# Splitting the last round's Fourier rows early, taking the second tile's statistic first, and giving all low parts of h to VectorE

## The chip, the cores and the metric

One core of a Trainium2 chip runs the whole kernel. The metric is the device time of one execution in microseconds (us). The kernel before was timed in three executions.

## The reference

A latent stream x (1024 tokens, width 1024) and a context stream (256 tokens) go through two layers. Cut to what bears on the change:

```
# layer 0, per stream; z = h @ w_in gives u, g, f, gf, each 1024 wide
r   = rglru_bidirectional(conv(u))                 # "r rows" of the mix
f   = fourier_mix(f, w_f, b_f)                     # "f rows" of the mix
mix = concatenate([r * silu(g), f * silu(gf)])     # 2048 wide
y   = mix @ w_out                                  # the first out-projection
x   = x + gate * rms_norm(y, g_post)
# layer 1 begins
h   = rms_norm(x, g_pre1) * (1 + scale1) + shift1
z   = h @ w_in1                                    # projections of layer 1
# then rotary, windowed attention with context keys, gate, out-projection, norm, residual
```

All of it is float32.

## The kernel before

**High and low parts.** TensorE takes each float32 operand as two parts of type fp32r, and every product is three matmuls: high by high, high by low, low by high. A high part is a copy with rounding by ScalarE (ACT); a low part is `raw - high`, a tensor_tensor by VectorE (DVE) or GpSimd (POOL). Most of what stands between a DMA and a matmul is this pair.

**Layer 0.** `mixers` (from L414) runs eight rounds, one for 128 channels each. A round makes one row block of r (tile `H` in the buffer `work`) and one of f (tile `xf`), and stores them to the DRAM tensor `mixT` (16 row blocks, of 128 channels by 1280 tokens). The body of the last round also starts the out-projection: L900 finishes f, L905 and L908 finish r, and between them stand calls of the out-projection's `weight_lo`.

**First out-projection** (`out_projection0`, L1118). Ten tiles of 128 tokens; each is a product of 16 blocks (8 of r, then 8 of f) of six matmuls, `half_product` (L1485) doing eight blocks. Tiles 0 and 1 are different: `first_pair` (L1459) walks the 16 weight rows in the order `K_ORDER` (L1109), which is r blocks 0 to 6, f blocks 0 to 6, then the last r block and the last f block, and tile 1 follows tile 0 at a distance of three blocks (`LAG`), so each weight row is split while PE works on others. Weight row i waits for `weight_lo(i)`. Block 7 in this order is the first that needs the f half of `mixT`: `ml[1]`.

Queues around it, each in program order:

- SP (DMA issues) loads the two r halves of tiles 0 and 1 (L1224, `load_first_mix`), weights 0 to 9, stores the last f rows (`store_f`), loads weight 10, waits until that store has landed, then loads the two f halves (L1239, L1240; all eight f row blocks from `mixT`), weight 11, `store_r`, and the rest. Each tile's raw rows use a slot of `mraw`.
- ACT: `weight_hi` 3 to 6, `mixed_hi(0, 1)` (tile 0, f half), `weight_hi` 7, `mixed_hi(1, 1)`, the last r rows straight from `H` (`last_r`), weights 8 to 15.
- DVE: weights 4 and 5, sum and product that finish r (L905, L908), then `weight_lo` 6, `mixed_lo(0, 1)`, 7, `mixed_lo(1, 1)`, `last_r`, 8 to 15.

After a tile's product comes its epilogue: ACT takes the sum of squares of Y and the root (L1315, L1317), DVE scales (L1375), POOL adds x (L1431), ACT takes the squares and the root again (L1323, L1325), DVE writes `xn` (L1386), PE transposes it to `TP` (L1502), DVE multiplies by the gain into `hb` (L1390), POOL adds the shift (L1433), SP stores h (L1213). The body of tile t on ACT and POOL is: split mix tile t+1 (r half, f half), then the epilogue of tile t-1. On SP: load mix tile t+1, load x tile t, store tile t-1; tile 3's mix is loaded by body 2, which comes after tile 0's h is stored. PE: the two half products of tile t, then the transposes of t-1.

**Projections of layer 1** (`projections1`, L1526). The stored h is read back in ten tiles through four slots; ACT makes `h_hi` (L1637), and the low parts are shared: tiles 2, 5 and 8 by POOL (L1743), the others by DVE (L1694), kept apart by `pool_share`, `dve_share` and `wait_low` (from L1091). Slot reuse waits for the low of the tile four back. PE's first slab product is cut in three chunks: tokens of tiles 0 to 3, 4 to 7, 8 and 9, each waiting for its lows. POOL also makes the lows of the first two weight slabs (L1732), the second one after h tile 5.

Of the kernel before, what the change touches and what calls it, by code (L numbers as in the profile page):

```python
# [413 lines left out]
def mixers(nc, a, h_hi, h_lo, work, cols, silu_c, gs, ident, mods, wraw, w_hi, w_lo, gf_hi, gf_lo, slab, W, W4, before,  # L414
           home, h1_ld, w1_ld):
    ctx = ExitStack()
    with ctx:
        def sb(name, shape, dt=F32):
# [44 lines left out]
        r7h, r7l = sem("last_r_hi"), sem("last_r_lo")  # L463
# [6 lines left out]
            nc, a, mods, home, ident, H, h1_ld, w1_ld,  # L470
            Freed(wl, s_gf, s_g, gp_, dft, mp, uv, us, yd, sg, mr, mf, mrs, mfs, gst, ge, r7h, r7l, slot_ld))
# [251 lines left out]
        def _(dve):  # L723
# [23 lines left out]
            def body(t, first, last):  # L747
# [367 lines left out]
Freed = namedtuple("Freed", "wl s_gf s_g gate_products dft mod_sums uv us yd sg mr mf mrs mfs gates_stored gate_rows r7_hi r7_lo slot_loaded")  # L1115


def out_projection0(nc, a, mods, home, ident, H, h1_ld, w1_ld, freed):  # L1118
# [42 lines left out]
    def loops(eng, body):  # L1161

        body(1, 1, False)
        with eng.Fori(1, LT // 2) as j:
# [14 lines left out]
    def sync(sp, store_f, store_r, store_gates):  # L1179
# [4 lines left out]
        def load_first_mix(t, h, slot):  # L1184
            n = KT - 1 if h == 0 else KT
            sp.dma_start(mraw[:, slot, 0:n], a["mixT"][h * KT:h * KT + n, :, t * P:(t + 1) * P]
                         .rearrange("k p n -> p k n")).then_inc(m_ld[slot], 16)
# [36 lines left out]
        load_first_mix(0, 0, 0)  # L1224
        load_first_mix(1, 0, 1)
# [25 lines left out]
        sp.wait_ge(freed.mrs, 16 * KT)  # L1251
        load_mix(2, 0)
# [24 lines left out]
    def scalar(act):  # L1277
        def mixed_hi(t, h):
            slot = t if h == 0 else 1 - t
            act.wait_ge(m_ld[slot], 16 * h + 16)  # L1280
# [4 lines left out]
            n = KT - 1 if h == 0 else KT  # L1285
            nc.scalar.activation(m_hi[t][:, h, 0:n], mraw[:, slot, 0:n], ACT.Copy).then_inc(mh[h], 1)

        def last_r():
            act.wait_ge(freed.mr, KT)
            for t in range(2):  # L1290
                nc.scalar.activation(m_hi[t][:, 0, KT - 1], H[:, t * P:(t + 1) * P], ACT.Copy).then_inc(freed.r7_hi, 1)

        def weight_hi(i):
# [5 lines left out]
            elif i == 10:  # L1299
                act.wait_ge(freed.r7_lo, 2)  # L1300
                act.wait_ge(freed.mrs, 16 * KT)
# [26 lines left out]
        def body(t, s, last):  # L1328
            if not last:
                split(t + 1, 1 - s, 0)  # L1330
                split(t + 1, 1 - s, 1)
            epilogue(t - 1, 1 - s)
# [16 lines left out]
    def vector(dve):  # L1349
# [6 lines left out]
        def mixed_lo(t, h):  # L1356
            slot = t if h == 0 else 1 - t
            n = KT - 1 if h == 0 else KT
            dve.wait_ge(mh[h], t + 1)
            tt(m_lo[t][:, h, 0:n], mraw[:, slot, 0:n], v32(m_hi[t][:, h, 0:n]), ALU.subtract).then_inc(ml[h], 1)  # L1360

        def last_r():
            for t in range(2):
                dve.wait_ge(freed.r7_hi, t + 1)
                tt(m_lo[t][:, 0, KT - 1], H[:, t * P:(t + 1) * P], v32(m_hi[t][:, 0, KT - 1]),
                   ALU.subtract).then_inc(freed.r7_lo, 1)
# [53 lines left out]
    def gpsimd(pool):  # L1420
# [6 lines left out]
        def epilogue(t, s):  # L1427
            w = 1 if is_ctx(t) else 0
            pool.wait_ge(x_ld, 16 * t + 16)
            pool.wait_ge(yn, t + 1)  # L1430
            tt(x1[:, s, :], x1[:, s, :], xt[:], ALU.add).then_inc(xd, 1)  # L1431
            pool.wait_ge(hg, t + 1)
            tt(hb[:, s], hb[:, s], mods[:, SHIFT1, w, :].unsqueeze(2).to_broadcast([P, KT, P]), ALU.add).then_inc(hd, 1)  # L1433

        def body(t, s, last):
            if not last:
                split(t + 1, 1 - s, 0)
                split(t + 1, 1 - s, 1)
            epilogue(t - 1, 1 - s)
# [7 lines left out]
    def tensor(pe, gate_rows):  # L1447
# [11 lines left out]
        def first_pair():  # L1459
            def step(t, i):  # L1460
# [8 lines left out]
                elif k == KT - 1:  # L1469
                    pe.wait_ge(freed.r7_lo, t + 1)  # L1470
                if t == 0:
# [54 lines left out]
def projections1(nc, a, kd_hi, kd_lo, vs, early, h_ld, w_ld):  # L1526

    ctx = ExitStack()
    with ctx:
# [20 lines left out]
        hh, hl = sem("h1_hi_done"), [sem("h1_lo0"), sem("h1_lo1")]  # L1550
# [29 lines left out]
        def _(sp):  # L1580
# [5 lines left out]
            for i in range(2, TT):  # L1586
                if i >= 4:
                    wait_low(sp, hl, i - 4)
# [3 lines left out]
            for i in range(TT - 4, TT):  # L1592
                wait_low(sp, hl, i)
# [133 lines left out]
        def _(pool):  # L1727
# [813 lines left out]
```

## Time and profile before

| | us |
|---|---|
| median of three executions | 1505.27 |
| lowest and highest | 1505.14, 1509.27 |
| the profiled execution | 1508.78 |
| its span, first to last instruction | 1507.0 |
| PE busy with matmuls | 1392.4 (92%) |
| DVE, ACT, POOL busy | 849.5, 736.1, 545.8 |
| mean granted TensorE clock | 0.974 |

Times in the rows are microseconds from the start of the span. A timeline row gives start, duration, engine, source line, operation, output and input, and in brackets the idle time ahead of it with what ended it. The profiled execution lies 1.8 us over its own span and 3.5 us (0.2%) over the median.

### The profile page before, as it was taken

Reading aid. Unit: us, or ns where it says so; the run is one execution under the profiler, and the core shown is the slowest. Engines: PE = TensorE matmul, PEld = TensorE weight load, DVE = VectorE, ACT = ScalarE, POOL = GpSimd, SP = SyncE. Lnnn points to the kernel's source line nnn. Section 1 sums busy time; section 2 is a strip of 40 time slices with the busy share of each in tenths; the row PEclk is TensorE's granted clock in tenths of the full one; section 3 lists DMA queues with packets and bytes.
Section 4 is the critical chain, followed back from the end, with each engine's and each line's share of the span. In section 5 each row is a group of like instructions: output and inputs, shape, how many; then the busy total and the mean of one; then the engine's idle time right before and its main releaser. Section 6 shows DMA issues by size and latency. Waiting matters only on the chain. (4 is left out here: it accounts for less than half of the span.)

```text
span 1507.0 us, 20164 instructions
## 1 busy us (share of the span) xinstructions
PE 1392.4 (92%) x7212; PEld 1161.1 (77%) x7212; DVE 849.5 (56%) x1231; ACT 736.1 (49%) x1149; POOL 545.8 (36%) x260
## 2 busy tenths in 40 slices
PE   5999999999999999989899957999996899998897
PEld 4778888888888888867788846888885788887676
DVE  7788767676776768751111225122221789997532
ACT  5475828273737464732122213222221899997511
POOL 0023232323222223203343414343542666667542
PEclk9999999999999999999999977999998999999999
DMA  9323122222121212372344334724335533241584
GB/s 380 138 70 111 60 92 72 79 75 90 61 90 61 90 61 78 116 252 83 114 115 120 98 110 171 182 84 139 111 104 140 177 121 106 77 147 52 178 231 125
DMA packets 94886, 179.45 MB, mean 119 GB/s; under 512 B 10448, under 2 KB 56944, under 8 KB 92528
## 3 DMA queue, kind: packets, MB, share of 16 engines
q1 hardware_dynamic: 94832, 178.74, 36.9%
q8 instruction: 33, 0.54, 0.2%
q14 instruction: 21, 0.17, 0.0%
HBM read 123.65 MB, written 45.11 MB: 112 GB/s over the span
## 5 line engine op out<-in xcount | busy, mean ns | idle before, releaser
L962 PE MATMUL slab<-h_hi,w_hi 128*128 128x512 f32 x720 | 258.0, 358 | 3.2 <-DVE h_lo L316 2.6
L964 PE MATMUL slab<-h_hi,w_lo 128*128 128x512 f32 x720 | 257.3, 357 | 0.0
L963 PE MATMUL slab<-h_lo,w_hi 128*128 128x512 f32 x720 | 257.2, 357 | 0.0
L931 POOL TENSOR_TENSOR w_lo<-wraw,w_hi 128x1024 fp32r<-128x1024 f32 x29 | 73.8, 2545 | 311.6 <-ACT w_hi L567 311.6
L2092 POOL TENSOR_TENSOR probs<-probs,rdenom 128x2560 f32<-128x2560 f32 (+1 forms) x32 | 135.7, 4241 | 58.1 <-DVE rdenom L2051 58.1
L962 PEld LDWEIGHTS slab<-h_hi,w_hi 128*128 128x128 f32 x720 | 135.5, 188 | 26.0 <-DVE h_lo L316 2.9
L1772 PE MATMUL slab<-h_hi,w_hi 128*128 128x512 f32 (+1 forms) x352 | 135.6, 385 | 18.9 <-DVE h_lo L1694 18.9
L963 PEld LDWEIGHTS slab<-h_lo,w_hi 128*128 128x128 f32 x720 | 135.5, 188 | 22.0
L964 PEld LDWEIGHTS slab<-h_hi,w_lo 128*128 128x128 f32 x720 | 135.5, 188 | 22.0
L1774 PE MATMUL slab<-h_hi,w_lo 128*128 128x512 f32 (+1 forms) x352 | 135.2, 384 | 0.0
L1773 PE MATMUL slab<-h_lo,w_hi 128*128 128x512 f32 (+1 forms) x352 | 135.1, 384 | 0.0
L2068 DVE TENSOR_TENSOR pt_lo<-TB,pt_hi 128x512 fp32r<-128x512 f32 x152 | 104.3, 686 | 32.8 <-ACT pt_hi L2010 26.5
L1970 ACT ACTIVATE probs<-probs,neg_max 128x640 f32<-128x640 f32 (+1 forms) x128 | 102.7, 802 | 23.2 <-DVE neg_max L2043 18.9
L2043 DVE CUSTOM_DVE_ANT_0 probs<-S,mask,nsink 128x640 f32<-128x640 f32 (+1 forms) x128 | 107.6, 842 | 1.7 <-PE S L2125 1.4
L743 DVE SCALAR_TENSOR_TENSOR E<-wm,silu_bcast 128x1024 f32<-128x1024 f32 x64 | 99.8, 1560 | 5.4 <-DMA wm<-in_wm 2.1
L2124 PE MATMUL S<-kd_hi,q_parts 128*128 128x256 f32 (+2 forms) x256 | 89.3, 353 | 13.4 <-DMA q_parts<-qT 12.3
L2164 PEld LDWEIGHTS TB<-ident,probs 128*128 128x128 f32 x608 | 75.9, 141 | 24.0 <-issue 3.7
L2164 PE MATMUL TB<-ident,probs 128*128 128x128 f32 x608 | 91.5, 273 | 2.9 <-DVE pt_lo L2068 1.5
L1772 PEld LDWEIGHTS slab<-h_hi,w_hi 128*128 128x128 f32 x352 | 67.3, 191 | 32.6 <-issue 16.7
L2010 ACT ACTIVATE pt_hi<-TB 128x512 fp32r<-128x512 f32 x152 | 89.2, 587 | 5.8 <-PE TB L2164 5.0
L1773 PEld LDWEIGHTS slab<-h_lo,w_hi 128*128 128x128 f32 x352 | 67.2, 191 | 12.8
L1774 PEld LDWEIGHTS slab<-h_hi,w_lo 128*128 128x128 f32 x352 | 67.1, 191 | 12.8
(321 smaller groups left out, 3184.2 us busy)
## 6 DMA issues: line engine op xcount, KB each, us to landing
wraw<-in_w_in SPq DMA_DIRECT2D x32, 512.0 KB, 3.3
wm<-in_wm SPq DMA_DIRECT2D x32, 512.0 KB, 3.5
mixT<-work SPq DMA_DIRECT2D x16, 640.0 KB, 4.0
mraw<-mixT SPq DMA_DIRECT2D x18, 512.0 KB, 5.4
wm<-in_wm SPq DMA_DIRECT2D x8, 1024.0 KB, 16.2
q_parts<-qT SPq DMA_DIRECT2D x32, 256.0 KB, 4.6
oT<-o_out SPq DMA_DIRECT2D x8, 1024.0 KB, 5.3
work<-in_xT SPq DMA_DIRECT2D x8, 640.0 KB, 8.6
```

The source lines that it names most:

```text
L743: nc.vector.scalar_tensor_tensor(out=E[:, 0:D], in0=wm1[:, q % 2, :], scalar=0.5, in1=silu_b[:, w, :], op0=ALU.mult, op1=ALU.mult, accum_o ...
L962: nc.tensor.matmul(out, l_hi, r_hi, start=start, stop=False)
L963: nc.tensor.matmul(out, l_hi, r_lo, start=False, stop=False)
L964: return nc.tensor.matmul(out, l_lo, r_hi, start=False, stop=stop)
L1772: nc.tensor.matmul(out, w_hi[:, j, k, :], rhs_hi, start=(k == 0), stop=False)
L1773: nc.tensor.matmul(out, w_hi[:, j, k, :], rhs_lo, start=False, stop=False)
L1774: last = nc.tensor.matmul(out, w_lo[:, j, k, :], rhs_hi, start=False, stop=(k == KT - 1))
L1970: nc.scalar.activation(r, r, ACT.Exp, bias=nm[:, u, h:h + 1], scale=-1.0, accum_out=rsum[:, u, h:h + 1]).then_inc(ed, 1)
L2043: nc.vector.tensor_tensor_reduce(out=row(b, pr[:, u, h, :]), in0=S[:, j % 2, at:768], in1=m, scale=-SCALE, scalar=nsink[:, j:j + 1], op0=A ...
L2068: tt(pt_lo[:, x, :], TB[:, tb_bank(b, u, x), :], v32(pt_hi[:, x, :]), ALU.subtract).then_inc(pl, 1)
L2092: nc.gpsimd.tensor_tensor(rows, rows, rden[:, u, :].unsqueeze(2).to_broadcast(rows.shape), ALU.mult).then_inc(pn, 1)
L2164: last = nc.tensor.transpose(TB[:, tb_bank(b, u, x), h * P:(h + 1) * P], pr[:, u, h, x * P:(x + 1) * P], ident[:])
```

## The change

Four edits.

1. In the last round the f halves of tiles 0 and 1 are also only seven row blocks, those stored by earlier rounds, so they no longer wait for the store of the last f rows. SP loads tile 0's f half right behind weight 2 and tile 1's behind weight 6. The eighth f rows come from `xf` as the eighth r rows come from `H` (`last_rows`, with semaphore `f7_lo`). ACT and DVE take these splits earlier: ACT after weights 4 and 5, DVE one between weights 4 and 5 inside the mixer's last round and one ahead of weight 6.
2. Body 1 of the epilogue loops: ACT takes the statistics of tiles 0 and 1 one behind the other, ahead of the split of tile 3; POOL adds x for tiles 0 and 1 ahead of the shift of tile 0. One more pair of bodies is written out for it.
3. SP's body t loads x tile t first, then mix tile t+2 (was t+1), then stores tile t-1.
4. All ten lows of h in `projections1` go to DVE, under one semaphore; POOL splits the second weight slab right behind the first.

```diff
@@ last round, VectorE
                     weight_lo(4)
+                    mixed_lo(0, 1)
                     weight_lo(5)
@@ SP
         load_w(2)
+        sp.wait_ge(m0l, 1)
+        sp.wait_ge(freed.mfs, 16 * (KT - 1))
+        load_first_mix(0, 1)
         sp.wait_ge(freed.s_g, 3 * KT)
-        for i in range(3, 10):
+        for i in range(3, 7):
+            load_w(i)
+        sp.wait_ge(ml[0], 1)
+        load_first_mix(1, 1)
+        for i in range(7, 10):
             load_w(i)
         store_f()
         load_w(10)
-        sp.wait_ge(freed.mfs, 16 * KT)
-        sp.wait_ge(m0l, 1)
-        sp.wait_ge(ml[0], 1)
-        load_first_mix(0, 1, 1)
-        load_first_mix(1, 1, 0)
         load_w(11)
         store_r()
...
         def body(t, s, last):
-            if not (isinstance(t, int) and t == 1) and not last:
-                load_mix(t + 1, 0)
-                load_mix(t + 1, 1)
             load_x(t)
+            if not (isinstance(t, int) and t >= TT - 2):
+                load_mix(t + 2, 0)
+                load_mix(t + 2, 1)
             store(t - 1, 1 - s)
@@ ScalarE
+        def last_rows():
+            act.wait_ge(freed.mf, KT)
             act.wait_ge(freed.mr, KT)
+            for h, rows in enumerate((H, xf)):
+                for t in range(2):
+                    nc.scalar.activation(m_hi[t][:, h, KT - 1], rows[:, t * P:(t + 1) * P],
+                                         ACT.Copy).then_inc(freed.rows_hi, 1)
...
         def body(t, s, last):
+            if isinstance(t, int) and t == 1:
+                split(2, 0, 0)
+                split(2, 0, 1)
+                epilogue(0, 0)
+                epilogue(1, 1)
+            else:
+                if not last:
+                    split(t + 1, 1 - s, 0)
+                    split(t + 1, 1 - s, 1)
+                if not (isinstance(t, int) and t == 2):
+                    epilogue(t - 1, 1 - s)
 
         def rest():
-            for i in range(3, 7):
+            weight_hi(3)
+            weight_hi(4)
+            mixed_hi(0, 1)
+            weight_hi(5)
+            mixed_hi(1, 1)
+            for i in range(6, 10):
                 weight_hi(i)
-            mixed_hi(0, 1)
-            weight_hi(7)
-            mixed_hi(1, 1)
-            last_r()
-            for i in range(8, K2):
+            last_rows()
+            for i in range(10, K2):
                 weight_hi(i)
@@ VectorE
         def rest(copy_gates):
-            weight_lo(6)
-            mixed_lo(0, 1)
-            weight_lo(7)
             mixed_lo(1, 1)
-            last_r()
-            for i in range(8, 12):
+            for i in range(6, 10):
+                weight_lo(i)
+            last_rows()
+            for i in range(10, 12):
                 weight_lo(i)
             copy_gates()
@@ GpSimd
+            if isinstance(t, int) and t == 1:
+                split(2, 0, 0)
+                split(2, 0, 1)
+                residual(0, 0)
+                residual(1, 1)
+                shifted(0, 0)
+            else:
+                if not last:
+                    split(t + 1, 1 - s, 0)
+                    split(t + 1, 1 - s, 1)
+                if not (isinstance(t, int) and t == 2):
+                    residual(t - 1, 1 - s)
+                shifted(t - 1, 1 - s)
@@ projections1, VectorE
-            for i in dve_share(TT):
+            for i in range(TT):
                 at = slice(i * P, (i + 1) * P)
                 dve.wait_ge(hh, i + 1)
-                tt(h_lo[:, :, at], h_tile(i), v32(h_hi[:, :, at]), ALU.subtract).then_inc(hl[1], 1)
+                tt(h_lo[:, :, at], h_tile(i), v32(h_hi[:, :, at]), ALU.subtract).then_inc(hl, 1)
@@ projections1, GpSimd
             split(0, 0)
-            for i in pool_share(TT):
-                at = slice(i * P, (i + 1) * P)
-                pool.wait_ge(hh, i + 1)
-                tt(h_lo[:, :, at], h_tile(i), v32(h_hi[:, :, at]), ALU.subtract).then_inc(hl[0], 1)
-                if i == 5:
-                    split(1, 0)
+            split(1, 0)
             pool.wait_ge(par, 48)
```

## Rows read from the trace of the kernel before

**Rows 1.** Waits by engine and line, PE, 600 to 950 us.

```profile
PE slab L1772 <- DVE h_lo L1694: 18.9, 2, 16.3
PE TP L1502 <- DVE xn L1386: 15.2, 2, 8.3
PE Y L1454 <- DVE wo_over_h L1354: 4.5, 1, 4.5
```

**Rows 2.** Windows: length, busy of PE, PEld, DVE, ACT, POOL, granted clock, DMA.

```profile
657.40:663.40 6.00, 6.00 (x14) 4.74 (x15) 5.93 (x7) 5.39 (x6) 0.00 (x0) 0.50 0.50 201
722.90:725.00 2.10, 2.10 (x7) 1.72 (x6) 1.23 (x1) 0.00 (x0) 0.36 (x1) 0.54 0.15 59
725.00:884.60 159.60, 159.60 (x716) 130.05 (x716) 23.82 (x34) 32.05 (x54) 58.08 (x26) 1.00 0.35 106
```

**Rows 3.** SP's timeline, the two f halves of the first pair.

```profile
649.49 1.00 SPq L1186 DMA_DIRECT2D mraw<-mixT  x2
```

**Rows 4.** VectorE's timeline in the first pair.

```profile
643.78 1.21 DVE L1354 TENSOR_TENSOR wo_over_h<-early,wo_over_h 128x1024 fp32r<-128x1024 f32 x1
...
648.11 1.22 DVE L1354 TENSOR_TENSOR wo_over_h<-early,wo_over_h 128x1024 fp32r<-128x1024 f32 x1
654.89 1.23 DVE L1360 TENSOR_TENSOR m_parts<-mraw,m_parts 128x1024 fp32r<-128x1024 f32 x1 [5.56 <-ACT m_parts L1286]
656.04 1.22 DVE L1354 TENSOR_TENSOR wo_over_h<-early,wo_over_h 128x1024 fp32r<-128x1024 f32 x1
```

**Rows 5.** PE's timeline, a stall in round 0 with its next matmul.

```profile
122.04 0.50 PE L962 MATMUL W<-pq_hi,ab_hi 128*128 128x512 f32 x1 [2.18 <-DVE pq_lo L873]
122.38 0.39 PE L963 MATMUL W<-pq_lo,ab_hi 128*128 128x512 f32 x1
```

**Rows 6.** PE's timeline, the transposes of tiles 1, 2 and 4.

```profile
721.33 1.97 PE L1502 MATMUL TP<-ident,xn 128*128 128x128 f32 x8 [8.32 <-DVE xn L1386]
...
746.11 1.03 PE L1502 MATMUL TP<-ident,xn 128*128 128x128 f32 x8
...
792.28 1.03 PE L1502 MATMUL TP<-ident,xn 128*128 128x128 f32 x8
```

**Rows 7.** Timelines of SP, ACT and POOL ahead of the stall at 721 us.

```profile
705.94 1.21 SPq L1195 DMA_DIRECT2D mraw<-mixT  x2
...
710.49 1.06 ACT L1310 ACTIVATE m_parts<-mraw 128x1024 fp32r<-128x1024 f32 x1 [16.91 <-DMA mraw<-mixT]
...
711.63 4.67 POOL L1425 TENSOR_TENSOR m_parts<-mraw,m_parts 128x1024 fp32r<-128x1024 f32 x2 [6.41 <-ACT m_parts L1310]
```

**Rows 8.** VectorE's timeline: hb of tile 0, scaling of tile 1, its xn.

```profile
702.02 1.22 DVE L1390 TENSOR_TENSOR hb<-TP,mods 128x1024 f32<-128x1024 f32 x1 [7.45 <-PE TP L1502]
...
714.92 1.28 DVE L1375 SCALAR_TENSOR_TENSOR x_tiles<-Y,st,gpb 128x1024 f32<-128x1024 f32 x1
...
720.52 0.75 DVE L1386 TENSOR_SCALAR xn<-x_tiles,st 128x1024 f32<-128x1024 f32 x1
```

**Rows 9.** A steady tile: its xn on DVE, the next mix split on ACT.

```profile
788.98 0.75 DVE L1386 TENSOR_SCALAR xn<-x_tiles,st 128x1024 f32<-128x1024 f32 x1
...
802.00 1.06 ACT L1310 ACTIVATE m_parts<-mraw 128x1024 fp32r<-128x1024 f32 x1 [13.26 <-DMA mraw<-mixT]
```

**Rows 10.** PE's timeline, chunks 0 and 1 of layer 1's first slab.

```profile
910.83 0.77 PE L1772 MATMUL slab<-h_hi,w_hi 128*128 128x512 f32 x1 [16.31 <-DVE h_lo L1694]
...
921.60 0.47 PE L1772 MATMUL slab<-h_hi,w_hi 128*128 128x512 f32 x1 [2.64 <-DVE h_lo L1694]
```

**Rows 11.** VectorE's timeline, the first two lows of h together.

```profile
903.74 5.82 DVE L1694 TENSOR_TENSOR h_lo<-early,h_hi 128x1024 fp32r<-128x1024 f32 x2 [6.70 <-ACT h_hi L1637]
```

**Rows 12.** Windows, the slow stretch in chunk 1 (columns as in rows 2).

```profile
922.80:926.30 3.50, 3.50 (x10) 2.70 (x9) 1.98 (x1) 0.00 (x0) 0.89 (x1) 0.51 0.14 36
```

**Rows 13.** Loads of h tiles: median landing; issue of tile 7; its high.

```profile
early<-hT SPq DMA_DIRECT2D x6, 512.0 KB, 4.2
...
910.71 0.33 SPq L1589 DMA_DIRECT2D rope_swap<-hT  x1
...
917.19 1.06 ACT L1637 ACTIVATE h_hi<-rope_swap 128x1024 fp32r<-128x1024 f32 x1 [1.36 <-DMA rope_swap<-hT]
```

More of the change, by code:

```diff
@@ L469, in mixers @@
         out_sync, out_scalar, out_vector, out_pool, out_tensor = out_projection0(
-            nc, a, mods, home, ident, H, h1_ld, w1_ld,
-            Freed(wl, s_gf, s_g, gp_, dft, mp, uv, us, yd, sg, mr, mf, mrs, mfs, gst, ge, r7h, r7l, slot_ld))
+            nc, a, mods, home, ident, H, xf, h1_ld, w1_ld,
+            Freed(wl, s_gf, s_g, gp_, dft, mp, uv, us, yd, sg, mr, mf, mrs, mfs, gst, ge, r7h, r7l, f7l, slot_ld))
         blk = ctx.enter_context(nc.Block())
@@ L1163, in loops @@
         body(1, 1, False)
-        with eng.Fori(1, LT // 2) as j:
+        body(2, 0, False)
+        body(3, 1, False)
+        with eng.Fori(2, LT // 2) as j:
             body(2 * j, 0, False)
@@ L1182, in at, with load_first_mix @@
             return t * P if isinstance(t, int) else sp.snap(t * P)
[L1184 to L1187, printed above, removed]
+        def load_first_mix(t, h):
+            n = KT - 1
+            sp.dma_start(mraw[:, t, 0:n], a["mixT"][h * KT:h * KT + n, :, t * P:(t + 1) * P]
+                         .rearrange("k p n -> p k n")).then_inc(m_ld[t], 16)
         def load_mix(t, h):
@@ L1223, in sync @@
         sp.wait_ge(freed.mrs, 16 * (KT - 1))
-        load_first_mix(0, 0, 0)
-        load_first_mix(1, 0, 1)
+        load_first_mix(0, 0)
+        load_first_mix(1, 0)
         sp.wait_ge(freed.s_gf, 3 * KT)
@@ L1251, in sync @@
         sp.wait_ge(freed.mrs, 16 * KT)
+        sp.wait_ge(freed.mfs, 16 * KT)
         load_mix(2, 0)
@@ L1278, in mixed_hi @@
         def mixed_hi(t, h):
-            slot = t if h == 0 else 1 - t
-            act.wait_ge(m_ld[slot], 16 * h + 16)
+            act.wait_ge(m_ld[t], 16 * h + 16)
             if t == 0:
@@ L1284, in mixed_hi @@
                 act.wait_ge(freed.mod_sums, 2 * N_MOD * KT)
-            n = KT - 1 if h == 0 else KT
-            nc.scalar.activation(m_hi[t][:, h, 0:n], mraw[:, slot, 0:n], ACT.Copy).then_inc(mh[h], 1)
-        def last_r():
+            n = KT - 1
+            nc.scalar.activation(m_hi[t][:, h, 0:n], mraw[:, t, 0:n], ACT.Copy).then_inc(mh[h], 1)
+        def last_rows():
+            act.wait_ge(freed.mf, KT)
             act.wait_ge(freed.mr, KT)
-            for t in range(2):
-                nc.scalar.activation(m_hi[t][:, 0, KT - 1], H[:, t * P:(t + 1) * P], ACT.Copy).then_inc(freed.r7_hi, 1)
+            for h, rows in enumerate((H, xf)):
+                for t in range(2):
+                    nc.scalar.activation(m_hi[t][:, h, KT - 1], rows[:, t * P:(t + 1) * P],
+                                         ACT.Copy).then_inc(freed.rows_hi, 1)
         def weight_hi(i):
@@ L1300, in weight_hi @@
                 act.wait_ge(freed.r7_lo, 2)
+                act.wait_ge(freed.f7_lo, 2)
                 act.wait_ge(freed.mrs, 16 * KT)
@@ L1356, in mixed_lo, with last_rows @@
         def mixed_lo(t, h):
-            slot = t if h == 0 else 1 - t
-            n = KT - 1 if h == 0 else KT
+            n = KT - 1
             dve.wait_ge(mh[h], t + 1)
[L1360 to L1366, printed above, removed]
+            tt(m_lo[t][:, h, 0:n], mraw[:, t, 0:n], v32(m_hi[t][:, h, 0:n]), ALU.subtract).then_inc(ml[h], 1)
+        def last_rows():
+            for h, (rows, done) in enumerate(((H, freed.r7_lo), (xf, freed.f7_lo))):
+                for t in range(2):
+                    dve.wait_ge(freed.rows_hi, 2 * h + t + 1)
+                    tt(m_lo[t][:, h, KT - 1], rows[:, t * P:(t + 1) * P], v32(m_hi[t][:, h, KT - 1]),
+                       ALU.subtract).then_inc(done, 1)
         def epilogue(t, s):
@@ L1425, in split, with residual @@
             tt(m_lo[s][:, h], mraw[:, h], v32(m_hi[s][:, h]), ALU.subtract).then_inc(ml[h], 1)
-        def epilogue(t, s):
-            w = 1 if is_ctx(t) else 0
+        def residual(t, s):
             pool.wait_ge(x_ld, 16 * t + 16)
@@ L1431, in epilogue, with shifted @@
             tt(x1[:, s, :], x1[:, s, :], xt[:], ALU.add).then_inc(xd, 1)
+        def shifted(t, s):
+            w = 1 if is_ctx(t) else 0
             pool.wait_ge(hg, t + 1)
@@ L1435, in body @@
         def body(t, s, last):
[L1436 to L1439, printed above, removed]
+            if isinstance(t, int) and t == 1:
[11 more added lines that the diff above has]
+                shifted(t - 1, 1 - s)
         pool.wait_ge(mh[0], 1)
@@ L1470, in step @@
                     pe.wait_ge(freed.r7_lo, t + 1)
+                elif k == K2 - 1:
+                    pe.wait_ge(freed.f7_lo, t + 1)
                 if t == 0:
@@ L1587, in _ @@
                 if i >= 4:
-                    wait_low(sp, hl, i - 4)
+                    sp.wait_ge(hl, i - 3)
                 sp.dma_start(h_tile(i), a["hT1"][i]).then_inc(h_ld[i % 4], 16)
@@ L1591, in _ @@
                     load_slab(1, 1, 0)
-            for i in range(TT - 4, TT):
-                wait_low(sp, hl, i)
+            sp.wait_ge(hl, TT)
             sp.dma_start(cos, a["rope"][0]).then_inc(par, 16)
@@ L1791, in _ @@
                     if s == 0:
-                        for i in range(at // P, (at + n) // P):
-                            wait_low(pe, hl, i)
+                        pe.wait_ge(hl, (at + n) // P)
                     if s >= 2:
```

12 lines of the change are left out of this document (4 added, 8 removed).

## The prediction, made before the changed kernel was run

> **What bounds the kernel now.** I looked first at the page's busy shares: PE is busy 92% of the span, so a gain can only come from places where PE stands still or runs at the lower clock. Next I read PE's waits in the stretch that the change touches [rows 1]. Three things stand there: 4.5 us in the first pair of tiles, waiting for a low part by VectorE; one wait of 8.3 us for the second tile's xn (the other wait of that line, 6.9 us, is the last tile's, and nothing is left to cover it; the change leaves it alone); and 18.9 us at the start of layer 1, of which 16.3 stand ahead of the first chunk and 2.6 ahead of the second. Then the windows behind each stall [rows 2, 12]: the granted clock is 0.50 for 6.0 us behind the first, 0.54 in a stretch behind the second and 0.51 for 3.5 us behind the last one, that is 1.2 GHz in place of 2.4. Between 725 and 884.6 us PE is busy all the time at clock 1.00. So these tiles are bound by PE, and every microsecond of stall removed is one off the end, until something else comes late. Behind the second of these chunks PE's timeline shows no idle, so a shift there is carried on.
>
> A stretch at half clock costs about half its length. It belongs to the stall ahead of it, and I count it with the stall.
>
> **Part 1, the first pair.** The stall is at block 7, the first that needs f rows. Its cause is on SP: both f halves are issued at 649.49 [rows 3], behind the store of the last f rows. The high comes when they land, DVE's low at 654.89, and weight 7, queued behind it on both engines, at 656.04 to 657.26; PE starts at 657.40 [rows 1, 4]. Of the stall's cost, 4.5 is idle and 3.0 is half of the 6.0 us at 0.50 [rows 2]: 7.5.
>
> After the change the f half of tile 0 needs only stored rows and is issued near 626 us, 24 us earlier, and tile 1's near 636. They add nothing to the bytes. What is late next? DVE's order. Before weight 6 it now has two m_parts splits of 7/8 of 1.23, about 1.1 each, 1.0 in pace since instructions overlap a little [rows 4]. Weight 5 moves from 643.78 to 644.8, done at 646.0; PE starts its block near 647.2, so that is hidden. Weight 6 ran at 648.11; it now runs at 650.1 and ends at 651.3. A block of six matmuls is 1.4 us at full clock (a tile of 16 blocks and 8 transposes is 23.08, half of 792.28 less 746.11 [rows 6]), and PE finished the two blocks from weight 6 on at 652.9, so it wanted weight 6 at 650.0. That makes a **new stall of 1.5 us** at block 6. Weight 7 then ends at 652.4, and PE reaches it at 651.5 plus two blocks, 654.3. After that each weight costs DVE 1.2 and PE 2.8 (two tiles), so the lead grows. The four short row splits (a quarter of a microsecond each) and weights 8 and 9 lie in it. The store of r rows leaves SP at 649 rather than 652, since the f halves no longer stand in its queue, so weight 10, which needs it landed, is not late: PE wants it near 663.
>
> Does PE's clock fall with a 1.5 us stall? This trace has a stall of 2.18 us with the next matmul 0.34 behind and no slow stretch after it [rows 5]; 4.5 us brought one. 1.5 is nearer to 2.18, and I take no loss; the other end is the 3.0 of before. The Trainium skill says, in "TensorE: Matmul & The Clock Gate", section "What's actually happening", that the throttled state is the default and activity releases it; by that an idle PE always risks the lower clock, and the sum would lose up to 3 us. Part 1 gives 7.5 - 1.5 = **6.0** (bounds 3.0 and 7.0, the last if weight 6 came only half a microsecond late).
>
> **Part 2, the second tile.** In the kernel before, SP loads mix tile 3 only at 705.94, behind the store of tile 0's h. ACT stands at the split of that tile for 16.91 us, to 710.49, with the statistic of tile 1 queued behind it, though Y of tile 1 was ready near 689.5 [rows 7]. xn comes at 721.27, PE idles 8.32 us [rows 6, 8]. The transposes then take 1.97 against 1.03, and from 721.33 to the next tile's transposes are 24.78 us against 23.08 in steady state [rows 6]: 1.7 for the clock. Together 10.0.
>
> After: the load of tile 3 goes out behind x tile 1, near 692.5; ACT has tile 1's first root by about 695. DVE still keeps its order, so tile 1's scaling follows hb of tile 0, which ends at 703.2 [rows 8]. With the reciprocal, 0.2, and 1.28 for the scaling it is ready at 704.7. From the end of the scaling to the end of xn were 716.2 to 721.3, 5.1 us [rows 8]: POOL's addition, ACT's square and root, DVE. POOL is free since the shift of tile 0 now stands behind. So xn is there at **709.8**, and PE wants it at 713.0 (721.33 less 8.32): 3.2 us of slack. Next in line is the low of tile 3's r half: ACT's high after the root at 708.8 to 709.9, POOL's shift of tile 0 (at most 2.4) from 707.2 to 709.1, then one POOL split of 2.34 [rows 7]: 712.4. PE wants it behind the transposes, near 713.8. Slack 1.4 us: hidden, and this is the tightest cover. The delayed shift and store of tile 0 (4 us later) have no reader before layer 1. Loads of mix tiles one body earlier land in a queue that carries 106 GB/s in these tiles [rows 2]. All of this moves with PE when part 1 shortens. Part 2 gives **10.0** (bounds 8.5 and 10.2).
>
> **Part 3, the rest of the loop.** PE is at 100% in steady state, so nothing is gained or lost: xn is ready at 789.7 and wanted at 792.28 [rows 6, 9], 2.6 us of slack, and ACT waits 13.26 us for mix rows [rows 9] that will now be there. Extra unrolled bodies of ACT, DVE, POOL and SP: nothing, their idle covers it.
>
> **Part 4, the lows of h.** The first two lows take 5.82 us [rows 11] where one alone takes 1.2. In that time POOL makes the low of the weight slab and of tile 2. So a DVE subtraction stands still while POOL runs one: 5.82 less 2 by 1.22 is 3.4 us of standing. This is the pattern that the Trainium skill gives in "SBUF — State Buffer", section "Who interferes with whom": a DVE instruction with two SBUF inputs contends with a GpSimd one that reads SBUF; the trace agrees, in size of an exclusive lock. Now: tile 0's low ends at 906.2 as before (POOL's slab split is still there), then tiles 1, 2 and 3 at 1.15 to 1.2 each: 909.7. Chunk 0 starts at 909.8 rather than 910.83 [rows 10]: 1.0. Chunk 0 took 8.1 us (910.83 to 918.96, that is 921.60 less 2.64), so PE wants chunk 1 at 917.9. Tile 7 is its last: its load waits for tile 3's low, 909.7. Landing is between the median 4.2 and the 6.5 that the same tile took (910.71 to 917.19) [rows 13]; then high 1.06 and low 1.3: between 916.3 and 918.6. I take 918.1, nearer to the late end since four loads follow each other here: chunk 1 starts 3.5 us earlier than at 921.60. Without the long stall the 3.5 us at 0.51 [rows 12] go too: 1.75. Loads 8 and 9 wait for the lows of tiles 4 and 5 and are needed only at chunk 2, 5.6 us on. POOL's second slab split runs near 909.6, beside DVE at the end of tile 3's low, and is not needed before slab 1. Part 4 gives **5.2** (bounds 2.0, if the clock falls again and the loads land late, and 5.8).
>
> **Sum.** 6.0 + 10.0 + 5.2 = 21.2. The profiled execution took 1508.8 (1507.0 of span and 1.8 around it) and would be 1487.6; the median is 3.5 lower, 1505.3, so I forecast 1505.3 - 21.2 = **1484**.
>
> **Rivals.**
> 1. *The clock falls in the new 1.5 us stall* and 6 us go at 0.50: 3 back, **1487**. For: each longer stall here brought it. Against: the 2.18 us stall without one [rows 5].
> 2. *Layer 1's tile loads land late*, as tile 7 did, and chunk 1 stalls enough for another slow stretch: 3.2 back, **1487**.
> 3. *The tile 3 low is late.* POOL adds x of tile 1 first, and only 1.4 us of slack are left; one POOL pass of 2.34 lost to contention with DVE costs 1 us, a late mix load more: 1485 to **1488**.
> 4. *Several covers thin at once*: two or three of these, **1490**.
> 5. *The other side, slower.* SP's body now waits for the lows of tile t+1 (needed to free mraw) ahead of storing tile t-1 and loading x of t+1. Were x late, tile after tile, xn would pass its slack of 2.6 us [rows 6, 9] in each of six tiles. To be over 1505.3 by 4.5 it must eat 21.2 + 4.5 = 25.7 in six tiles, 4.3 each, so x would have to be 6.9 us late in each: **1510**. Against it: the lows are made in the first half of a tile's 23 us, and x is asked for ahead of the mix rows.
> 6. *The edit doesn't act*: the f halves are issued early but ACT reaches them no sooner. Then part 1 gives nothing: **1490**. DVE stood idle 5.56 us ahead of the old split, waiting for it [rows 4], which speaks against it.
>
> **How the numbers follow.** Forecast 0.55, with its own range 1482 to 1486. Rivals 1 and 2 0.11 each, rival 3 0.08, 4 and 6 0.06 together, 5 0.02; 0.07 for more than forecast (weight 6 not late and all upper bounds: 7.0 + 10.2 + 5.8 = 23.0, 1482, and below by the scatter of the medians). The range, 1480 to 1490, reaches from there to where rivals 4 and 6 begin. 0.3% is 4.5 us, about what a measurement of this kernel tells from no change: faster by more than that in all cases but rival 5 and some untold mishap: 0.96; same 0.02; slower 0.02.
>
> **What would show it.** Part 1: the PE wait of 4.5 us is gone, one of about 1.5 us stands at weight 6, and the clock behind it is 1.00. Part 2: the 8.3 us wait for xn is gone and the waits for xn hold only the last tile's 6.9; all transposes but the last take 1.03. Part 4: single lows of 1.2 us on DVE but for the first; chunk 0 a microsecond earlier against the last transposes; a wait of under 1 us at chunk 1. The prediction is wrong if the clock falls in the new stall, if PE waits for a low by POOL at tile 3, or if chunk 1 waits 2 us or more.

## The result, and the profile after

The changed kernel takes **1491.7 us** (median of four, 1491.3 to 1495.5), the kernel before 1507.0 beside it: ratio 0.990, 95% interval 0.988 to 0.992. In a second set it took 1490.7 against 1506.7. So it is faster by 15 to 16 us; I had forecast 21, and 1484. The range, 1480 to 1490, missed. Of the 7.7 us between 1484 and 1491.7, 1.7 are the starting point: I subtracted from 1505.3, the median of three executions, and this set has 1507.0. The other 6 are gain that wasn't there.

| | before | after |
|---|---|---|
| median here, us | 1507.0 | 1491.7 |
| profiled execution; its span | 1508.8; 1507.0 | 1495.5; 1493.6 |
| PE busy | 1392.4 (92%) | 1387.8 (93%) |
| mean granted clock | 0.974 | 0.979 |

The profiled execution of after lies 4 us over its median, that of before 2 us over the median of this set.

Waits by engine and line of the changed kernel, PE, 600 to 1160 us (us in total, times, longest); left out are two lines of the attention behind the projections and one of 0.3 that before has too.

```profile
PE slab L1796 <- DVE h_lo L1723: 16.8, 2, 15.3
PE TP L1532 <- DVE xn L1404: 6.9, 1, 6.9
PE VP L1808 <- DVE vs L1743: 3.0, 2, 2.0
PE Y L1482 <- DVE wo_over_h L1372: 1.3, 1, 1.3
PE W L963 <- ACT work L587: 1.1, 1, 1.1
PE slab L1796 <- POOL w_lo L1761: 0.8, 1, 0.8
PE Y L1482 <- DVE x_tiles L1393: 0.4, 1, 0.4
```

Against [rows 1]: 4.5 us for a weight low have become 1.3; of 15.2 for xn only the last tile's 6.9 is left; 18.9 for lows of h have become 16.8. But three lines are larger than they were or new: 3.0 us in the transposes of v (VP), where before had 2.0, 0.8 for a weight low by GpSimd, and 0.4 ahead of tile 2, where PE now waits for the scaling of tile 0.

Where do the 13.4 us of the two profiled spans lie? I compare PE's timelines from a common mark, the first product of the last round's Fourier transform (616.64 before, 616.81 after). To the last tile's transposes before has 275.9 us, after 260.1: **15.8 gained**, 16.0 forecast. From there to the end of layer 1's slabs before has 259.05, after 260.0: **0.9 lost**, 5.2 gain forecast. The rest, the mark's own 0.2 and 1.3 behind the slabs, is within what fourteen profiles scatter there (355.1 to 356.9 us from the slabs to the end). The whole miss, at first look, is in part 4. But the 0.9 is of one pair of executions: a second profile of the changed kernel (e5 below) has 257.5 for this piece, a second one of before (e14 below) 258.0. So over these pairs part 4 is between 2 us lost and 1.5 gained.

The first pair, SP's, VectorE's and PE's timelines of the changed kernel:

```profile
625.59 0.38 SPq L1189 DMA_DIRECT2D mraw<-mixT  x1
...
636.40 0.55 SPq L1189 DMA_DIRECT2D mraw<-mixT  x1
```

```profile
643.92 1.08 DVE L1377 TENSOR_TENSOR m_parts<-mraw,m_parts 128x896 fp32r<-128x896 f32 x1
...
649.26 1.08 DVE L1377 TENSOR_TENSOR m_parts<-mraw,m_parts 128x896 fp32r<-128x896 f32 x1
650.26 2.35 DVE L1372 TENSOR_TENSOR wo_over_h<-early,wo_over_h 128x1024 fp32r<-128x1024 f32 x2
```

```profile
651.53 0.50 PE L1482 MATMUL Y<-wo_over_h,m_parts 128*128 128x512 f32 x1 [1.30 <-DVE wo_over_h L1372]
651.87 0.39 PE L1483 MATMUL Y<-wo_over_h,m_parts 128*128 128x512 f32 x1
```

The loads go out at 626 and 636, the two splits stand ahead of weight 6, and PE waits 1.30 us there, as worked out ahead (1.5). The next matmul comes 0.34 behind: the clock hasn't fallen. The second tile's part also came as drawn, in VectorE's timeline:

```profile
697.87 1.28 DVE L1393 SCALAR_TENSOR_TENSOR x_tiles<-Y,st,gpb 128x1024 f32<-128x1024 f32 x1
703.25 0.16 DVE L1400 RECIPROCAL st<-st 128x1 f32<-128x1 f32 x1 [4.10 <-ACT st L1334]
703.45 0.75 DVE L1404 TENSOR_SCALAR xn<-x_tiles,st 128x1024 f32<-128x1024 f32 x1
```

xn is there 5.05 us behind the end of the scaling and PE doesn't wait for it.

The start of layer 1, timelines of VectorE, SP and ScalarE, then PE's in the transposes of v:

```profile
888.11 3.66 DVE L1723 TENSOR_TENSOR h_lo<-early,h_hi 128x1024 fp32r<-128x1024 f32 x2 [6.70 <-ACT h_hi L1666]
```

```profile
894.07 0.33 SPq L1619 DMA_DIRECT2D rope_swap<-hT  x1
...
947.63 0.89 SPq L1614 DMA_DIRECT2D early<-in_w_in  x1
```

```profile
901.28 1.06 ACT L1666 ACTIVATE h_hi<-rope_swap 128x1024 fp32r<-128x1024 f32 x1 [1.72 <-DMA rope_swap<-hT]
...
954.19 1.06 ACT L1661 ACTIVATE w_hi<-early 128x1024 fp32r<-128x1024 f32 x1 [11.51 <-DMA early<-in_w_in]
955.15 1.06 ACT L1687 ACTIVATE vs<-VP 128x512 fp32r<-128x512 f32 x2
```

```profile
956.51 0.44 PE L1808 MATMUL VP<-ident,rope_in 128*128 128x128 f32 x2 [2.04 <-DVE vs L1743]
```

The first two lows take 3.66 us where they took 5.82 [rows 11], and chunk 0 starts 17.27 us behind the last transposes, before 18.28: the 1.0 us of the forecast. Tile 7's load took 7.2 us from issue to its high (894.07 to 901.28), so chunk 1 waited 1.5. And 50 us later something new stands. ScalarE waits 11.51 us for weight slab 4 (it waited 11.78 before, too), but now the copy of the v rows, queued behind, is late for PE: 2.04 us of wait where before had 0.97. A window of PE behind it (columns as in [rows 2]):

```profile
957.70:964.00 6.30, 6.27 (x15) 4.92 (x16) 0.12 (x1) 1.85 (x4) 2.37 (x1) 0.50 0.40 116
```

6.3 us at 1.2 GHz, about half of it lost (14 matmuls of 512 columns, 0.43 us each from start to start in place of 0.23).

### The profile page after: what moved, and what is told of

The parts are those of the page before. It is cut to its first block and busy times, and to the rows that moved or that the text cites. A ratio compares the mean times of both kernels' runs of the same rounds, so it can differ in the third digit from the quotient of the medians.

```text
span 1493.6 us, 20128 instructions
## 1 busy us (share of the span) xinstructions
PE 1387.8 (93%) x7212; PEld 1157.6 (78%) x7212; DVE 847.4 (57%) x1236; ACT 736.0 (49%) x1151; POOL 536.6 (36%) x257
## 5 line engine op out<-in xcount | busy, mean ns | idle before, releaser
L1796 PE MATMUL slab<-h_hi,w_hi 128*128 128x512 f32 (+1 forms) x352 | 136.3, 387 | 17.6 <-DVE h_lo L1723 16.8
```

The lines of the kernel that those rows point to most:

```text
L1796: nc.tensor.matmul(out, w_hi[:, j, k, :], rhs_hi, start=(k == 0), stop=False)
```

## Experiments

All times are medians on one chip for a set, with the kernel before at 1507.5 in the first set (e1 to e4), 1506.7 in the second (e5 to e8) and 1507.1 in the third (e11 to e13). The changed kernel's 1491.7 is from a set of its own, with 1507.0 beside it. Single executions of one kernel lie up to 7 us apart, and with 4 or 5 of them per kernel I estimate a difference of two medians as uncertain by 2 to 3 us. So what an edit is worth is read from PE's timeline as well, which agrees to 0.1 us where no slow stretch differs.

**The fourth edit undone**, `e1_lows_shared`: `projections1` as before, the rest as changed.

> The changed kernel with its fourth edit undone: the lows of h shared between VectorE and GpSimd as before, the rest as changed. Theory: the whole gain of this edit (3.9 us at the start of chunk 1: 1.0 ahead of chunk 0 and 2.9 ahead of chunk 1, less the slow stretch behind it) is lost again some 50 us later, because the loads of weight slabs 2 and 3 and the rotation that follows them come only with the lows: 2.0 us instead of 1.0 in the transposes of v, 0.8 for a weight low, and 2.7 for a slow stretch. So undoing it costs nothing: time within 2 us of the changed kernel's 1491.5 (1490 to 1493), with PE's waits in the transposes of v back to 1.0 each and no slow stretch behind them. Rival, that the edit is worth its 5 us: 1496 to 1497.

1492.6 us (ratio 0.990, 0.9885 to 0.9914). Against 1491.7 and 1490.7 for the changed kernel in its two sets, the edit with its VectorE lows is worth 1 to 2 us and not 5, not clear of nothing. From the last transposes to the end of the slabs its trace has 260.0 us, where the changed kernel has 260.0 and 257.5. The waits in the transposes of v are back at 1.0 each. From the last transposes to the first ones of v are 81.5 us here and 76.5 in the changed kernel's first profile, so 5.0 are gained at the front, and in that pair all of it is given back behind. (Chunk 1 waited 3.5 here, longer than in either profile of before.)

**The first edit undone**, `e3_first_pair_as_before`.

> The changed kernel with its first edit undone: the f halves of tiles 0 and 1 are loaded whole, behind the store of the last f rows, as before; the rest as changed. Theory: the first pair's 4.5 us wait and the 6 us at half clock come back, the 1.3 us wait goes: 5.9 us slower than the changed kernel, 1497 to 1498. Rival, that part of it was hidden behind the later stalls: under 4 us.

1494.9 us (ratio 0.992, 0.9903 to 0.9938): 3.2 us over the changed kernel by the medians, which here are no more than a hint, and 3.7 from mark to last transposes, which is clear. The rival's number, not mine. PE's waits and two windows of this kernel:

```profile
PE Y L1474 <- DVE wo_over_h L1363: 3.8, 1, 3.8
```

```profile
654.80:658.80 4.00, 3.98 (x11) 3.15 (x12) 4.00 (x6) 3.74 (x5) 0.00 (x0) 0.57 0.78 316
658.80:662.00 3.20, 3.20 (x15) 2.50 (x14) 1.95 (x2) 1.83 (x2) 0.00 (x0) 1.00 0.00 0
```

But nothing is hidden behind later stalls, as the rival had it: the same wait is 3.8 here in place of 4.5, and behind it 8 matmuls are slow in place of 14. The wait of 0.4 ahead of tile 2 is gone too: it stands in every kernel here with the first edit and in none without, and I had put it at nothing. The sum closes: 3.8 and 1.6 (8 matmuls at 0.2), less 1.3 and 0.4, is 3.7. The size of the term was off, not its place.

**The kernel before, once more**, `e14_before_again`.

> The kernel before, unedited, in a second profiled execution. The question is the size of the clock's terms: in the first one 14 matmuls (6.0 us) ran at half clock behind the 4.5 us wait of the first pair, and 4 behind the wait for the second tile. Theory, that the length of a slow stretch is not a property of the stall but of the execution: the lengths differ here, between 6 and 14 matmuls behind the first wait. Rival, that each is fixed by its stall: 13 to 14 and 4 again.

One profiled execution, 1506.1 us (the same kernel beside it 1504.0). PE's wait in the first pair and the windows behind it and behind the second tile's wait:

```profile
PE Y L1454 <- DVE wo_over_h L1354: 3.4, 1, 3.4
```

```profile
656.60:659.90 3.30, 3.30 (x9) 2.59 (x8) 3.30 (x6) 3.27 (x4) 0.00 (x0) 0.52 0.76 309
720.80:724.90 4.10, 4.10 (x12) 3.16 (x11) 1.07 (x1) 0.00 (x0) 1.90 (x1) 0.53 0.02 6
```

Here 7 matmuls were slow behind the first wait and 10 behind the second; in the profile I predicted from it was 14 and 4. The first wait also differs in length, 3.4 against 4.5, so by itself it doesn't tell whether the stall or the execution sets the slow stretch. The second does: 8.5 against 8.3, and 10 against 4. In this execution the first pair's part is worth 3.4 + 1.4 - 1.3 - 0.4 = 3.1, and from the mark to the first tile's transposes PE's timelines give 3.3 (82.0 less 78.7), close to what e3 shows.

**The second and third edits undone**, `e4_statistic_as_before`.

> The changed kernel with its second and third edits undone: bodies and mix loads in the old order, tile 3's mix loaded behind the store of tile 0's h. Theory: the 8.3 us wait for the second tile's xn and 1.7 us of slow clock come back, 10 us slower than the changed kernel: 1501 to 1502. Rival, that the first edit alone, by having loads earlier, removes part of it: under 8 us.

1502.9 us (ratio 0.997, 0.9960 to 0.9983): 11.3 over the changed kernel, and 11.3 from mark to last transposes too. Its wait for the second tile's xn:

```profile
PE TP L1512 <- DVE xn L1395: 15.4, 2, 8.5
```

8.5 us of it, 6.9 being the last tile's, and behind it transposes and 9 matmuls at half clock, where the profile before had 4. The forecast of 10.0 was low for the same reason for which the first was high.

**Weight slabs 2 and 3 loaded first**, `e2_slab_loads_first`.

```diff
-            sp.wait_ge(hl, TT)
-            sp.dma_start(cos, a["rope"][0]).then_inc(par, 16)
-            ...
             load_slab(2, 0, 1)
             load_slab(3, 1, 1)
+            sp.wait_ge(hl, TT)
+            sp.dma_start(cos, a["rope"][0]).then_inc(par, 16)
+            ...
```

> The changed kernel, with the loads of weight slabs 2 and 3 of layer 1 issued ahead of the wait for all lows of h and ahead of the rope tables, in place of behind them. Theory: ScalarE then doesn't wait 2.2 us for slab 2, GpSimd reaches the sines 2 us earlier, the sixteen copies of k leave SP 2 us earlier, weight slab 4 lands 2 us earlier, and the 2.05 us wait in the transposes of v goes back to 1.0, without the 0.8 us wait and the slow stretch behind it: 4 us faster than the changed kernel, 1487 to 1488. Rival A, that the chain is bound elsewhere (PE's chunk 2 or the rope tables): no change, 1491 to 1492. Rival B, that the tables now come late by as much: the wait moves to VectorE's rotation and the time stays.

1489.0 us (ratio 0.988, 0.9866 to 0.9901), 1 us over what I expected and 1.6 to 2.6 under the changed kernel. The longer wait for v is 1.0, there is no slow stretch behind it, and the piece from last transposes to end of slabs is 254.0 us, 5.0 and 4.0 less than in the two profiles of the kernel before. Some of that is not this edit: chunk 1 didn't wait in this execution, where the changed kernel waited 1.5 and 0.6. The first copy of k leaves SP 43.6 us behind the start of the last transposes, in the changed kernel's two profiles 46.6 and 45.0.

**Sines ahead of the weight low on GpSimd**, `e8_sines_first`.

```diff
-                split(s, 1)
                 sines(s)
+                split(s, 1)
```

> The changed kernel with GpSimd's sines ahead of its weight low in the rotation of k, the slab loads left where the change has them. Theory: what made PE wait in the transposes of v is the chain rotation, copies of k, load of weight slab 4, and not slab 2 as such; taking 2.4 us out of this chain at another place then removes the same 2.0 us wait and its slow stretch: 1487 to 1489, like e2_slab_loads_first. Rival: it was the slab loads' place in SP's queue alone; then 1491 to 1492, unchanged.

1490.3 us, the changed kernel beside it 1490.7: unchanged, which is the rival's number, and the wait for v is 1.5. The trace says why, and it says nothing on the chain. VectorE's and GpSimd's timelines:

```profile
915.35 3.31 DVE L1736 TENSOR_TENSOR rope_in<-rope_cosined,rope_swap 128x1024 f32<-128x1024 f32 x1 [2.67 <-POOL rope_swap L1766]
```

```profile
912.84 2.39 POOL L1766 TENSOR_TENSOR rope_swap<-rope_swap,early 128x1024 f32<-128x1024 f32 x1 [18.66 <-DVE rope_swap L1732]
915.18 2.40 POOL L1761 TENSOR_TENSOR w_lo<-early,w_hi 128x1024 fp32r<-128x1024 f32 x1
```

The weight low moved from ahead of the rotation to beside VectorE's sum, and that sum takes 3.31 us where it took 1.23: of 2.4 us taken out of the chain 2.1 came back into it. It neither supports nor refutes the chain. It does show the standstill of part 4 a second time: VectorE ends 1.1 us, most of one operation, behind GpSimd.

**Slab 4's load ahead of the second copies**, `e11_slab4_load_first`, and the same with shared lows, `e13_shared_slab4_first`.

```diff
             for s in range(2):
+                if s == 1:
+                    load_slab(4, 0, 2)
+                    load_slab(5, 1, 2)
                 for ready, part, dst in ((rh, H, kd_hi), (rl, L, kd_lo)):
...
             def body(t, first, last):
-                load_slab(2 * t + 4, 0, t + 2)
-                load_slab(2 * t + 5, 1, t + 2)
+                if not first:
+                    load_slab(2 * t + 4, 0, t + 2)
+                    load_slab(2 * t + 5, 1, t + 2)
```

> The changed kernel with one edit: the loads of weight slabs 4 and 5 stand on SP ahead of the eight copies of the second k slab, not behind all sixteen. Theory: the wait of 1.6 to 2.0 us in the transposes of v comes from ScalarE, which stands at the high of slab 4 until its load lands, with the copy of the v rows queued behind; the load was late because it stands behind copies that take SP 18 us. With the load earlier, ScalarE doesn't wait, both waits for v are 1.0, the 0.8 us wait for slab 4's low and the slow stretch behind are gone: 1487 to 1488. Rival: SP's copies themselves, which the rotated rows wait for, hold the chain; then 1491, unchanged.

> The same edit with the lows of h shared between VectorE and GpSimd as before the change (as e1_lows_shared). Theory: in e1_lows_shared the load of slab 4 wasn't late for PE, so this stays at 1491 to 1493, and the distance to e11_slab4_load_first, 4 to 5 us, is what the fourth edit is worth where nothing behind it takes it back. Rival, that the edit itself is worth next to nothing: within 1.5 us of e11_slab4_load_first.

This is the direct test, since the rotation and the copies keep their places. 1488.3 us (ratio 0.988, 0.9858 to 0.9896) with VectorE's lows, 1493.5 (0.992, 0.9901 to 0.9934) with shared ones: **5.2 us apart**, where without this edit the two are 1 to 2 us apart. That this is just the forecast's 5.2 is luck: the two medians are of 4 and 5 executions (1485.9 to 1489.7 and 1490.9 to 1496.8), and the two profiles are 3.8 apart from the last transposes to the end of the slabs (254.7 and 258.5) and 3.6 in all. So the edit is worth some 4 to 5 us here, clearly more than nothing. PE's waits in layer 1 of e11, and ScalarE's copy of v, which waits for PE and no more for a load:

```profile
PE VP L1812 <- DVE vs L1747: 2.0, 2, 1.0
PE slab L1800 <- DVE h_lo L1727: 1.2, 1, 1.2
```

```profile
940.16 1.07 ACT L1665 ACTIVATE w_hi<-early 128x1024 fp32r<-128x1024 f32 x1
952.50 1.09 ACT L1691 ACTIVATE vs<-VP 128x512 fp32r<-128x512 f32 x2 [11.27 <-PE VP L1812]
```

**The changed kernel again, and two refinements.**

> The changed kernel once more, beside the others of this set, to compare with them on one chip. Expected: 1491 to 1493 and 15 us under the kernel before; in its profile, a wait of 1.3 us at weight 6, and in layer 1 one of 0 to 2 us at chunk 1, since that one was 1.5 in the first profile and absent in others with the same code there.

1490.7 us, with waits of 1.3 at weight 6, 0.6 at chunk 1, 1.6 for v and 0.8 for the weight low; 7 slow matmuls behind these where the first profile had 14, which is 1.4 us at 0.2 each. With the shorter waits the piece from last transposes to end of slabs is 257.5 us, 2.5 less than in the first profile of the same kernel: between two executions, a difference as large as my smaller terms. The first profile, at 1495.5, is 4 us over the kernel's median, and this one, at 1490.2, is near it.

> Slab loads first (as e2_slab_loads_first), and VectorE's order in the first pair changed: weights 6 and 7 ahead of the f split of tile 1. Theory: the 1.3 us wait at weight 6 is the one m_parts split of 1.0 us in front of it, so it goes to 0.3 and PE's span shortens by 1.0 against e2_slab_loads_first. Rival: tile 1's block 7 then waits for its f low by as much, and nothing is gained.

1487.8 us. VectorE's weights 6 and 7 stand ahead of the split:

```profile
PE Y L1484 <- DVE wo_over_h L1372: 0.3, 1, 0.3
```

1.3 us have become 0.3, and from mark to last transposes are 259.1 us in place of 260.1, so the wait was the one split, and tile 1's block 7 didn't wait for it. e2 itself took 1489.0 in its own set; the 1.2 us between the two are what was expected, but across sets.

> Slab loads first, and seven raw slots for the h tiles in place of four (the buffers of the gate and of the rotated rows, idle at that time), so that the loads of tiles 4 to 6 wait for no low and tile 7's waits for tile 0's. Theory: the wait at chunk 1 is the landing of tile 7 and is gone in every profile (VectorE's low of tile 7 done at least 2 us ahead of PE's end of chunk 0); up to 1.5 us less than e2_slab_loads_first, and nothing where that had no wait. Rival: more loads in flight make tiles 2 and 3 land later, chunk 0 starts later, and nothing is gained or the time is 1 us worse.

1488.6 us: no wait at chunk 1 (e6 beside it, with four slots, had 1.8 there). The size isn't what I wrote. Tile 7 is still late, ScalarE's timeline has its high at the start of this pair:

```profile
900.09 2.19 ACT L1667 ACTIVATE h_hi<-early 128x1024 fp32r<-128x1024 f32 x2 [1.73 <-DMA early<-hT]
```

Its low ends about when PE ends chunk 0, not 2 us ahead. In time the edit can't be told from e2.

> The changed kernel with all that helped or should: slab 2 and 3 loads first, slab 4 and 5 loads ahead of the second copies, seven slots for h tiles, VectorE's weights 6 and 7 ahead of tile 1's f split. Theory: waits at weight 6, at chunk 1 and for slab 4 are all gone, 4.5 to 5.5 us under the changed kernel: 1486 to 1487. Rival: the covers overlap and it is no better than e6_weights_before_split, 1488.

1487.4 us (ratio 0.987, 0.9852 to 0.9886), PE's waits from weight 6 to the end of layer 1's slabs all gone but 0.3 at weight 6, 0.4 ahead of tile 2, the last tile's 6.9, 15.3 ahead of chunk 0 and 2 by 1.0 for v. 3.3 to 4.3 us under the changed kernel, where I expected 4.5 to 5.5, and the fastest version run. It is not clear of e6 at 1487.8 or e11 at 1488.3, so the rival, that the covers overlap, isn't refuted.

## Why the prediction was right or wrong

**What bounds the kernel**: right. Every stall removed in the first out-projection came off the end.

**Part 1, the first pair**: mechanism right, size wrong. The new wait at weight 6 was 1.3 (1.5 said), the clock held, the store of r rows and weight 10 weren't late. For the execution that I read, the working was nearly right: from the mark to the first tile's transposes before has 84.3 us and after 78.7, so 5.6 for 6.0; what is missing is the 0.4 that stands new ahead of tile 2. But in other executions the whole is worth 3.3 (e14) and 3.7 us (e3). The step that failed is the size of the stall and its slow stretch, 4.5 + 3.0, taken from one execution: two others with this code in the first pair have 3.8 and 4.0 us slow, 3.4 and 3.3 us slow, so 5 to 6 in place of 7.5. Why the wait itself varies from 3.4 to 4.5 is not shown.

**Part 2, the second tile**: right, and worth 11.3 (10.0 said; 10.2 in the profile that it was read from). xn and tile 3's low both came in time, so rival 3 is refuted. The 1.7 for the clock was at its low end in that one profile (24.78 us from these transposes to the next); it was 2.8 and 2.6 in the two others, e14 and e4 (25.90 and 25.71).

The two errors go against each other, since in the profile I read the slow stretch was long in one place and short in the other: the sum, 16.0, was measured as 15.8 between the two profiled executions, and as 14.7 between the changed kernel and the before of e14 (274.85 from mark to last transposes there, less 260.11). That it came so close is in part luck.

**Part 3, the loop**: right. PE is busy throughout, with 23.09 us from one tile's transposes to the next; the slower rival 5 doesn't occur.

**Part 4, the lows of h**: the local sum was near, the carry was wrong. Worked out to the start of chunk 1 it was at the good end of the scatter (chunk 0 1.0 earlier as said; chunk 1 waits 1.5, 0.6, 1.9, 1.8, 1.2, 0.8 or not at all in the kernels with this code, where I took 0.2; the bound from tile 7's landing, 6.5, was exceeded: 7.2). My own sign, a wait of under 1 us at chunk 1, was missed in the first profile and met in e5. e11 against e13 gives 3.8 (profiles) to 5.2 (medians) for it. The step that failed is the sentence that a shift is carried on because **PE's timeline shows no idle** behind the second chunk. That is PE's present state, not the slack of what feeds it. A second chain runs beside PE there: loads of slabs 2 and 3, rotation, sixteen copies of k that take 18.6 us of SP's queue, then the load of slab 4, whose high on ScalarE stands ahead of the copy of v. It starts from the last low of h, and moved by less than PE. SP's and ScalarE's timelines of the kernel before, and PE's wait there, show what slack there was:

```profile
964.94 1.73 SPq L1584 DMA_DIRECT2D early<-in_w_in  x1
```

```profile
971.73 1.06 ACT L1632 ACTIVATE w_hi<-early 128x1024 fp32r<-128x1024 f32 x1 [11.78 <-DMA early<-in_w_in]
973.61 1.08 ACT L1658 ACTIVATE vs<-VP 128x512 fp32r<-128x512 f32 x2 [0.82 <-PE VP L1784]
```

```profile
PE VP L1784 <- DVE vs L1714: 2.0, 2, 1.0
```

ScalarE waited 11.78 us for slab 4, then, with that done, 0.82 us for PE: a slack of 0.8 (0.3 in e14). Counted from the start of the last transposes, PE reached the first ones of v 3.9 us earlier than before (76.5 for 80.4), slab 4's high came only 1.9 us earlier (77.3 for 79.2). 2.0 less a slack of 0.8 is 1.2, and the wait for v grew by 1.1. With 0.8 for the weight low behind it and 14 slow matmuls (2.8), that took back 4.7 where 3.9 had been gained, and 0.9 is the measured loss. In e5's profile it was 0.6 + 0.8 + 1.4 = 2.8 of 4.6, and 1.5 is the measured gain. e11 shows that this is the cause: with slab 4's load ahead of the second copies ScalarE no longer waits for it, and the piece takes 254.7 us.

In the medians: 3.2 + 11.3 + 0.9, the steps from e3, e4 and e1 to the changed kernel, is 15.4, which is the whole difference. Against the forecast -2.8, +1.3 and -4.3. That they add up to the tenth is luck, since each step is uncertain by 2 to 3 us.

**Rivals and range.** Rival 2, a wait at chunk 1 long enough for another slow stretch, didn't occur in the changed kernel's two profiles but did in e4 and e6, whose code is the same there (waits of 1.9 and 1.8, then 7 and 8 slow matmuls). None of the rivals had the gain of part 4 given back behind the stretch I looked at. The range was also narrower than its own bounds: 3.0, 8.5 and 2.0, the low ends of the three parts, make 13.5 and a time of 1491.8, and I had cut it off at 1490. With part 4 at nothing and the other two as forecast it would be 1489.3 from my starting point and 1491.0 from this set's 1507.0.

## What to carry to other kernels

Where a stall on the bound engine is removed, look at the slack of every other engine and queue for as far as the shift is to be carried: the smallest slack of a feeder (here 0.8 us in one execution and 0.3 in another, ScalarE's copy of v behind a load) bounds what is carried on without loss, and "no idle" on the bound engine says nothing of it. A load whose slot is free long ago should not stand behind stores and copies in one in-order queue, and a wait at the head of an in-order engine holds work that was ready. A term for the clock belongs in a sum as a range over executions, not as one trace has it, and the stall in front of it too.

## What the runs showed of the hardware

The length of a stretch at half clock behind one and the same stall differs from one execution to the next. Behind the second tile's wait (8.3, 8.5 and 8.5 us in before, e14 and e4) 4, 10 and 9 matmuls of 512 columns were slow. The wait ahead of chunk 0 was 15.3 us in ten profiles, and 7 to 14 were slow behind it. Behind the first pair's wait it was 14, 7 and 8, with waits of 4.5, 3.4 and 3.8. A slow matmul takes 0.43 us from start to start in place of 0.23, so the difference is worth up to 1.4 us in either direction, as much as a small edit.

Waits of 1.3 us at weight 6 never lowered the clock in a profile here, nor did those of 0.6 to 1.5 at chunk 1 (after, e5, e8, e11); those of 1.8 (e6) and 1.9 (e4) at chunk 1 were followed by 8 and 7 slow matmuls, and the longer ones there (2.2 to 3.5, lows shared) by 7 to 14, though 2.2 us in round 0 were not [rows 5]. In the transposes of v a wait of 1.5 to 2.0 us with one of 0.8 behind it was followed by 7 to 14. So between 1.5 and 3.4 us the length of the wait alone doesn't tell.

A VectorE tensor_tensor with both inputs in SBUF stands still beside a GpSimd tensor_tensor: two lows 5.82 us beside two GpSimd operations, 3.66 beside one, 3.31 for one sum that takes 1.23 alone. So giving VectorE more of these operations can make its own work end earlier (with all ten lows of h in place of seven it ends the last one 29.4 and 29.1 us behind the start of the last transposes in the two profiles, where the two engines together ended at 32.2 and 30.8), and moving a GpSimd operation beside one can cost as much as it saves. The Trainium skill says in "SBUF — State Buffer", section "Who interferes with whom", that a DVE instruction with two SBUF inputs contends with a GpSimd instruction that reads SBUF. The traces agree, with the numbers above.
